# Four norms that sum partly on VectorE, and two modulation steps that move to a later layer

## The reference

```python
def rmsnorm(x, g):
    xf = x.astype(jnp.float32)
    y = xf * lax.rsqrt(jnp.mean(xf * xf, axis=-1, keepdims=True) + EPS)
    return (y * g.astype(jnp.float32)).astype(x.dtype)

# first block
x = x + o @ w_out[l]                              # OUT1
h = rmsnorm(x, ffn_norm_g[l])                     # norm 1
u = causal_dwconv(h @ w_up[l], ...)               # UP1
x = x + (jax.nn.silu(gate) * val) @ w_down[l]     # DOWN1
# second block, two layers i
mod = sc @ w_ada[i] + b_ada[i]                    # the modulation
h = modulate(x, norm_mix[i], sh_m, sc_m)          # norm 2 (i=0), norm 4 (i=1)
x = x + g_m[:, None, :] * y                       # OUT2, OUT3
h = modulate(x, norm_ffn[i], sh_f, sc_f)          # norm 3 (i=0), norm 5 (i=1)
x = x + g_f[:, None, :] * swiglu(h, w_gate_up[i], w_down[i])   # UP2, DOWN2, UP3, DOWN3
```

## Time and profile before

| What | Value |
|---|---|
| Median of 3 runs | 913.37 us |
| Lowest and highest run | 910.86 and 913.92 us |
| Span of the profiled execution, first to last instruction | 909.7 us |
| TensorE busy | 900.3 us (99%) |
| VectorE busy | 749.3 us (82%) |
| ScalarE busy | 503.3 us (55%) |
| GpSimd busy | 49.5 us (5%) |
| Granted TensorE clock over the span | 1.000 |

### The profile page before, as it was taken

The page is one execution under the profiler, slowest core; times in us unless marked ns, Lnnn a source line. Parts: engine busy times, 40 slices in busy tenths (PEclk is TensorE's granted clock), DMA queues, the critical chain, the costliest instruction groups (busy, mean ns, idle before and its releaser), DMA issues.

```text
span 909.7 us, 18262 instructions
## 1 busy us (share of the span) xinstructions
PE 900.3 (99%) x7367; PEld 875.8 (96%) x7367; DVE 749.3 (82%) x1032; ACT 503.3 (55%) x776; POOL 49.5 (5%) x87
## 2 busy tenths in 40 slices
PE   8999999999999999999999999999999999999998
PEld 7999999999999989999999999999999999999886
DVE  6999989999899789898987887987998887667544
ACT  6446757666665467764754444436645564444531
POOL 5100000000001000010000100100000000000000
PEclk9999999999999999999999999999999999999999
DMA  9887375666667947575469988984687467664541
GB/s 288 281 282 270 115 244 197 220 222 207 231 232 278 325 137 255 169 268 192 139 205 325 335 301 314 328 268 149 199 280 260 139 229 251 235 213 180 186 139 47
DMA packets 132129, 207.71 MB, mean 228 GB/s; under 512 B 4711, under 2 KB 109537, under 8 KB 126945
## 3 DMA queue, kind: packets, MB, share of 16 engines
q1 hardware_dynamic: 123968, 156.47, 51.3%
q0 software_dynamic: 8064, 50.34, 15.9%
q10 hardware_dynamic: 32, 0.01, 0.0%
HBM read 205.75 MB, written 1.05 MB: 227 GB/s over the span
## 4 chain that ended last, share of the span: by engine, by line
PE 91%; DVE 5%; ACT 2%; issue 1%; DMA 1%; SPq 0%; ACTq 0%; DVEq 0%
PE bank L1673 25%; PE bank L1675 25%; PE bank L1674 25%; PE bank L1828 2%; PE bank L1744 2%; PE bank L1753 2%; PE bank L1742 2%; PE bank L1710 1%; PE bank L1718 1%; PE bank L1712 1%; DVE w_lo L1002 1%; DMA w_raw<-in_w_in 1%; ACT w_hi L582 1%; PE bank L2028 0%; PE bank L2157 0%
## 5 line engine op out<-in xcount | busy, mean ns | idle before, releaser
L1002 DVE TENSOR_TENSOR w_lo<-w_raw,w_hi 128x1024 fp32r<-128x1024 f32 x294 | 353.8, 1221 | 107.6 <-ACT w_hi L582 105.4
L582 ACT ACTIVATE w_hi<-w_raw 128x1024 fp32r<-128x1024 f32 x293 | 306.1, 1056 | 242.3 <-PE bank L1675 226.7
L1673 PE MATMUL bank<-act_hi,w_hi 128*128 128x256 f32 x1312 | 366.1, 279 | 0.1
L1675 PE MATMUL bank<-act_hi,w_lo 128*128 128x256 f32 x1312 | 363.0, 277 | 0.0
L1674 PE MATMUL bank<-act_lo,w_hi 128*128 128x256 f32 x1312 | 363.0, 277 | 0.0
L1673 PEld LDWEIGHTS bank<-act_hi,w_hi 128*128 128x128 f32 x1312 | 246.5, 188 | 0.7 <-issue 0.6
L1674 PEld LDWEIGHTS bank<-act_lo,w_hi 128*128 128x128 f32 x1312 | 246.6, 188 | 0.4 <-issue 0.2
L1675 PEld LDWEIGHTS bank<-act_hi,w_lo 128*128 128x128 f32 x1312 | 246.6, 188 | 0.0
L1018 DVE SCALAR_TENSOR_TENSOR ada_acc<-ada_raw,silu_c,ada_acc 128x2048 f32<-128x2048 f32 (+1 forms) x56 | 114.3, 2040 | 1.7 <-DMA ada_raw<-in_w_ada 1.4
L1673 PE MATMUL bank<-hid_hi,w_hi 128*128 128x256 f32 x352 | 98.2, 279 | 0.0
L1674 PE MATMUL bank<-hid_lo,w_hi 128*128 128x256 f32 x352 | 97.2, 276 | 0.0
(11 more groups left out here) (309 smaller groups left out, 1374.0 us busy)
## 6 DMA issues: line engine op xcount, KB each, us to landing
w_raw<-in_w_gate_up SPq DMA_DIRECT2D x44, 1024.0 KB, 5.2
ada_raw<-in_w_ada POOLq DMA_DIRECT2D x40, 1024.0 KB, 5.3
w_raw<-in_w_down SPq DMA_DIRECT2D x33, 1024.0 KB, 5.1
w_raw<-in_w_in SPq DMA_DIRECT2D x23, 1024.0 KB, 6.8
w_raw<-in_w_up SPq DMA_DIRECT2D x22, 1024.0 KB, 5.7
w_raw<-in_w_qkv SPq DMA_DIRECT2D x12, 1024.0 KB, 7.3
w_raw<-in_w_out SPq DMA_DIRECT2D x8, 1024.0 KB, 7.0
ada_raw<-in_w_ada POOLq DMA_DIRECT2D x16, 512.0 KB, 4.9
```

Of the source, the lines that this page charges most:

```text
L582: act.activation(unit(w_hi, u), raw_half(c, h), ACT.Copy).then_inc(hi_ready, 1)
L1002: dve.tensor_tensor(unit(w_lo, u), raw_half(c, h), unit(w_hi, u).bitcast(F32), ALU.subtract).then_inc(lo_ready, 1)
L1673: pe.matmul(dst, a_hi, b_hi, start=start, stop=False, skip_group_check=True)
L1675: return pe.matmul(dst, a_lo, b_hi, start=False, stop=stop, skip_group_check=True)
```

## The change

1. In norms 1, 3, 4 and 5 VectorE adds the squared tiles 2 and 3, and then 4 and 5, to tiles 0 and 1 (`add_squares`, two instructions of 128x512 per norm, with a new semaphore `sq_added`). TensorE then sums four tiles (0, 1, 6, 7) and not eight. Norm 2 stays as it was.
2. TensorE does the four sums together after tile 5 of the first raw chunk. Before, six lay among the last products of OUT1, OUT2 and OUT3 and two after tile 2 (for norm 4 four lay at the end of DOWN2, two after tile 0, two after tile 2).
3. In `add_up` the first addition comes ahead of split (0, 1), the second after the last update of the residual. All eight `raw_lower` come after it, and split (1, 0) after these. Before, three `raw_lower` and split (1, 0) came ahead of the last update. In DOWN2 the additions follow the updates of banks 2 and 3, and all `raw_lower` come at the end.
4. Modulation steps 8 and 9 leave VectorE's stretch between OUT1's last split and `add_up`. The steps in UP1 are numbered down by two (8, 9, 10 in place of 10, 11, 12), and DOWN1 has seven steps, in rows 0, 1, 2, 3, 4, 6 and 8, in place of five, in rows 1, 3, 4, 6 and 8.

```diff
-ADA_OUT1, ADA_AT2_0, ADA_IN3 = 8, 18, 42
-ADA_UP = {UP1: {3: (10,), 6: (11,), 9: (12,)},
+ADA_AT2_0, ADA_IN3 = 18, 42
+ADA_UP = {UP1: {3: (8,), 6: (9,), 9: (10,)},
-ADA_DOWN = {DOWN1: {1: 13, 3: 14, 4: 15, 6: 16, 8: 17}, DOWN2: {0: 36, 1: 37, 3: 38, 5: 39, 6: 40, 8: 41}}
+ADA_DOWN = {DOWN1: {0: 11, 1: 12, 2: 13, 3: 14, 4: 15, 6: 16, 8: 17}, DOWN2: {0: 36, 1: 37, 3: 38, 5: 39, 6: 40, 8: 41}}
...
                     else:
+                        add_squares(n, 0)
                         split_unit(c0 + 4, 1)
-                        raw_lower(n, range(3))
-                        split_unit(c0 + 5, 0)
                         dve.wait_ge(unit_done, 2 * (c0 + 3) + 2)
                     update(bank[OUT_BANKS[c0][j]], j, gate)
-                raw_lower(n, range(3, KT))
+                add_squares(n, 1)
+                raw_lower(n, range(KT))
+                split_unit(c0 + 5, 0)
+
+            def add_squares(n, step):
+
+                dve.wait_ge(sq_ready, 5 * (n - 1) + 2 + step)
+                if step:
+                    dve.wait_ge(sq_added, 2 * RAW_INDEX[n] + 1)
+                dve.tensor_tensor(scr[:, 0:2, :], scr[:, 0:2, :], scr[:, 2 + 2 * step:4 + 2 * step, :], ALU.add
+                                  ).then_inc(sq_added, 1)
...
-                    if c0 == DOWN2:
-                        raw_lower(4, ((), (0, 1), (2,), range(3, KT))[j])
+                    if c0 == DOWN2 and j > 1:
+                        add_squares(4, j - 2)
+                if c0 == DOWN2:
+                    raw_lower(4, range(KT))
...
-            for n in range(2):
-                ada(ADA_OUT1 + n)
             stack_up()
             add_up(OUT1)
...
-                    if arrives and n == 4 and k == 0:
-                        square_part(4, 2)
-                    if arrives and k == 2:
+                    if arrives and k == 5:
+                        square_part(n, 0)
                         square_rest(n, 3)
...
-                        if n == 3 and outputs[0] == 2 and r < 1:
-                            square_part(NORM_AFTER[c0], r + 2)
...
-                pe.wait_ge(sq_ready, 5 * (n - 1) + part + 1)
+                if part == 0 and n in RAW_INDEX:
+                    pe.wait_ge(sq_added, 2 * RAW_INDEX[n] + 2)
+                else:
+                    pe.wait_ge(sq_ready, 5 * (n - 1) + part + 1)
...
-                    if (h, j) in ((0, 3), (1, 2)):
-                        square_part(NORM_AFTER[c0], h)
+                    if c0 == DOWN1 and (h, j) in ((0, 3), (1, 2)):
+                        square_part(2, h)
```

More of the change, by code:

```diff
@@ L280, in model_kernel @@
         sq_ready = sem("sq_ready")
+        sq_added = sem("sq_added")
         ss_ready = sem("ss_ready")
```

## The result

The changed kernel takes 920.84 us (median of 16 runs; 15 of them lie between 912.4 and 926.7, one at 2321), the kernel before on the same chip 913.09 (16 runs, 910.9 to 913.9). The ratio is 1.0071, with a 95% interval of 1.005 to 1.0092: slower by 0.7%, above the range of the prediction. The spread is a result too: 14 us against 3.

The account below looks back on a forecast made before the run. TensorE, busy 99% of the span, was taken as the bound. A loss of 2.1 us in DOWN1 less a gain of 0.9 in the norms gave +1.2 on 913.4, so 914.6 us; range 910.5 to 917.5.

Parts of the forecast that it names:

- The norms: Norms 1, 3, 4 and 5: fewer sums gain 0.5, 0.15, 0 and 0.2 us, 0.9 together, of a 6.9 us ceiling.
- The chain to (2, 1): VectorE's work from the last residual update to split (2, 1) limits each norm's gain; usable leads 0.70, 1.07, 0, 1.08 us.
- the first rival: TensorE's saving of 6.9 us from fewer sums in the four norms comes through in full: 908.6 us; chance 0.12.
- The addition's price: Each 128x512 fp32 addition on VectorE in the norms costs 0.60 us, bounds 0.60 and 0.69.
- The wait for the additions: TensorE's sums after tile 5 find the additions done, lead 0.4 to about 1 us, so costed at nothing.
- DOWN1: Two added modulation steps make TensorE wait 1.8 us at (2, 1) and 0.3 at (4, 1): cost 2.1 us.
- Nothing regains it: In DOWN1, TensorE's waits from the moved modulation steps are not made up later, since TensorE is the bound: 2.1 us.
- the 3.7 us from span to median: Whole kernel before: the median lies 3.7 us above the profiled span of 909.7, so the forecast was added to 913.4.
- The full saving: TensorE's 6.9 us from fewer sums in the norms gained entirely: 908.6, or 906.5 with no DOWN1 stall; chance 0.12.
- the missing stall in DOWN1: VectorE enters DOWN1 with over 2.3 us more lead, so TensorE doesn't stall: 912.5 us; chance 0.10.
- the third, slower: VectorE's backlog in DOWN1 falls on TensorE in full, 4.5 us; with no gain in the norms 917.9; chance 0.16.

Follow-up runs that it names:

- e1: Changed kernel with the modulation steps back where they were, so only sums and norm order change: 916.30 us, ratio 1.0025 to the kernel before.
- e2: Kernel before with only the two modulation steps moved, sums as they were: 916.44 us, ratio 1.0024.
- e5: Changed kernel plus one plain fp32 matmul of 4 columns in five places: 915.14 us, ratio 1.0028 to the kernel before.
- e10: Changed kernel plus a 4-column matmul on rounded operands in the same five places as e5: 925.36 us, ratio 1.0132 to the kernel before.
- e3: Kernel before with the split of unit (4, 1) of UP1 computed twice, so that it comes late: 913.75 us, ratio 0.9996.
- e7: Kernel before with only half of the split of unit (4, 1) of UP1 computed twice: 912.25 us, ratio 1.0.
- e9: Kernel before plus one plain fp32 matmul of 4 columns after chunk 2 of IN3: 911.92 us, ratio 0.9986.
- e8: Changed kernel with norm work moved to ScalarE, earlier splits and a new one-column tile that shifts later tiles: 918.91 us, ratio 1.0081 to the kernel before.
- e17: Kernel before with an unused tile of 32 columns, so that later tiles lie 128 bytes further: 926.03 us, ratio 1.0156.
- e12: e11 with tiles back in place and each plain fp32 matmul behind the waits of its place: 909.51 us, ratio 0.997 to the kernel before.
- e15: e12 with UP1's plain fp32 matmul replaced by four, between two chunks of every second pair: 909.93 us, ratio 0.9983 to the kernel before.
- e11: e8 plus nine plain fp32 matmuls of 4 columns: 919.46 us, ratio 1.0061 to the kernel before.

## Why the prediction was wrong

**The norms: right.** The chain to (2, 1) binds as worked out. In norm 1 TensorE breaks off for 0.56 and 0.54 us at (2, 0) and (2, 1), 1.1 together where 1.2 was given. It comes to (2, 1) at 153.66, 1.46 us earlier than in the earlier trace rows; 0.5 of this was there already at 120 us, before the change begins, and 0.4 is pace again: the last 100 products of OUT1 are slow in the kernel before and fast in the changed one. The two together are why the first raw chunk starts at 137.99, not at 138.95. What is left for the norm is 0.5, as given. In norms 3 and 5 the breaks sum to 1.39 and 1.33 us (1.57 and 1.5 were given), in norm 4 to 0.99 and 0.47 at the splits (0.9 and 0.6) and 0.57 for `raw_hi` (0.2). Each wait costs some 0.11 us more than these figures, since the matmul behind the first one starts 0.22 us after it and not 0.11 (279.59 and 279.81 above); the prediction has no such term. In e1, with the long layers fast, the sums bring 0.2 us of a ceiling of 6.9. The Trainium skill (Perfetto Trace Analysis, Identifying the Most-Contended Engine) says to optimize the engine with the highest occupancy first. Read as the first rival reads it, that gives 6.9 us here, and no run shows it.

**The addition's price: right.** L1128 starts at 138.86 and the next instruction at 139.46: 0.60 us, as taken.

**The wait for the additions: right.** It is in no list of waits.

**DOWN1: right in mechanism and size.** 1.8 and 0.3 us were given. e2 shows 1.78, and e5's profile shows 1.78 and 0.26. In the changed kernel's own profile they are 0.88 and 0.26; TensorE came there at the slow pace, which left VectorE more time.

**The step that failed** is the one that the sum took without a word: that each matmul left in the stream lasts as long as before. "Nothing regains it" was said of a wait as if its length were its whole price, and the range had no term for anything else. It measured 9.4 us in the profiled execution (some 2110 matmuls at 117.8 ns in place of 113.3); the terms that the sum did have came to about +0.5 (0.9 gained up to and in the norms, 0.4 of it by OUT1's pace, and 1.4 lost in DOWN1) where +1.2 was given, and the half microsecond from the first 9 us of the program was luck. The waits that the change brings are breaks in TensorE's stream, and each slow stretch in the changed kernel's profile begins at one. A wait of 0.08 us stood before a loss of 4.3 us (958 matmuls). That the pace makes the loss, and not the length of the waits, is shown by e5, which leaves all waits in place, sets the pace, and has 5.7 us of the median back; and by e10, which left the slow pace in all five places and loses 4.5 us more. That the change's new waits are what starts the slow stretches is less well shown: e1, with the waits of the norms, spreads up to 925.3 us, but its profiled run has them all and stays fast, and e3 and e7, with one such wait added, were slow in one run of 25. What decides at a break stays open.

**The range and the chances.** The spread of the kernel before, 3 us, was taken as noise that can't be told apart. It was the same effect: two levels 2.3 us apart, of which e9 removes the upper one with one instruction. So were the 3.7 us from span to median: in every run that has both, the time lies only 1.6 to 2.0 us above its own span, so the profiled execution was one of the lower level. Tracing the two levels to a layer would have suggested that the same could happen to others.

**The rivals.** The full saving and the missing stall in DOWN1 didn't occur. The result lies on the side of the third, slower, but not by its mechanism: (4, 1) of DOWN1 lost 0.3 us.

## What to carry to other kernels

Before adding up waits, count the matmuls that the engine which sets the time runs in equal windows without a wait, in both kernels: if they differ at the same granted clock, the waits explain only a part. A spread of runs in levels is a finding to be traced to its stretch, not noise, and a profile belongs to one run: compare it with that run's time, not with the median. When a tile is added for an experiment, put it where it moves no other tile, or the experiment measures the move as well.

## What the runs showed of the hardware

- At a granted clock of 1.00 (the level of 2.4 GHz) TensorE's matmuls of 256 columns, each with its own weights, go at 113.3 or at 117.8 ns from start to start. The Trainium skill (TensorE: Matmul & The Clock Gate, Wait — 56ns, not 53.3ns?) gives the columns over 2.4 GHz plus about 2.5 ns, from which I estimate 109.2 ns for 256 columns; both paces here are longer, and the measurement decides.
- In the 14 profiles whose tiles lie where they did before, the pace of these products changes only at a break; with moved tiles it also changes without one (e8, e17). A plain fp32 matmul of 4 columns in a running stream left the fast pace in every profiled place of e5, e9, e12 and e15 that has these products behind it, five of which had been slow up to it, and the slow pace in the one place of e12 where it stood right behind a wait, and of e11 where a wait stood right behind it; a rounded one left the slow pace in five of five, all fast up to it. What in TensorE keeps the pace isn't known.
- With the streamed tiles moved by 32 or 64 bytes it was 118.3 or 120.0 ns. The Trainium skill (SBUF — State Buffer, Operand start alignment) asks only for a multiple of the element size and says that this is about legality, not speed; here 32 bytes cost 17 us of 912.
